# Two stacked transformer blocks on one core: the steps of all engines in another order, with matmuls on one part of the array more often together

## The reference

```python
def first_block(x, ...):
    for layer in range(2):
        h = rms_norm(x, pre_norm[layer])
        m = even_mixer(h, ...) if layer % 2 == 0 else odd_mixer(h, ...)
        x = x + rms_norm(m, post_norm[layer])

def even_mixer(h, positions, w_in, w_out):
    (aq, ak, av, ag, iq, ik, iw, bq, bk, bv, bg) = split_columns(h @ w_in, EVEN_WIDTHS)
    a = dsa_attention(...) * jax.nn.silu(ag)
    r = head_group_norm(retention(...)) * jax.nn.silu(bg)
    return jnp.concatenate([a, r], axis=-1) @ w_out
```

## Time and profile before

| | |
|---|---|
| time, median of 3 runs | 866.23 us (866.14 to 866.57) |
| span of the profiled execution, first to last instruction | 864.6 us |
| TensorE, matmuls | 855.4 us busy, 99% of the span |
| TensorE, weight loads (beside matmuls) | 725.5 us |
| VectorE | 671.9 us, 78% |
| ScalarE | 489.5 us, 57% |
| GpSimd | 40.3 us, 5% |
| transfers | 155.12 MB, 179 GB/s on average |
| granted TensorE clock | 0.999 of full speed |

### The profile page before, as it was taken

The page is one execution under the profiler, slowest core; times in us unless marked ns, Lnnn a source line. Parts: engine busy times, 40 slices in busy tenths (PEclk is TensorE's granted clock), DMA queues, the critical chain, the costliest instruction groups (busy, mean ns, idle before and its releaser), DMA issues.

```text
span 864.6 us, 13438 instructions
## 1 busy us (share of the span) xinstructions
PE 855.4 (99%) x5062; PEld 725.5 (84%) x5062; DVE 671.9 (78%) x1238; ACT 489.5 (57%) x905; POOL 40.3 (5%) x72
## 2 busy tenths in 40 slices
...
GB/s 328 287 240 150 167 80 194 137 221 222 167 99 228 268 219 49 77 111 179 172 202 212 174 193 228 188 131 251 115 159 146 146 195 221 169 220 213 216 155 49
DMA packets 46748, 155.12 MB, mean 179 GB/s; under 512 B 5500, under 2 KB 8668, under 8 KB 46684
## 3 DMA queue, kind: packets, MB, share of 16 engines
...
...
## 4 chain that ended last, share of the span: by engine, by line
PE 97%; DVE 1%; ACT 1%; DMA 0%; issue 0%; SPq 0%; POOL 0%; DVEq 0%
PE ps L2161 17%; PE ps L2189 14%; PE ps L797 12%; PE ps L973 10%; PE ps L2169 9%; PE ps L809 6%; PE ps L861 5%; PE ps L872 4%; PE ps L864 4%; PE ps L1062 4%; PE ps L1119 3%; PE ps L1071 3%; PE ps L905 1%; PE ps L800 1%; PE ps L801 1%; DMA raw<-in_ws 0%
## 5 line engine op out<-in xcount | busy, mean ns | idle before, releaser
L769 DVE TENSOR_TENSOR wlo<-raw,whi 128x1024 fp32r<-128x1024 f32 (+1 forms) x262 | 311.1, 1216 | 56.6 <-ACT whi L762 55.3
L762 ACT ACTIVATE whi<-raw 128x1024 fp32r<-128x1024 f32 x261 | 266.6, 1049 | 115.9 <-DMA raw<-in_ws 37.1
L2161 PE MATMUL ps<-t,whi 128*128 128x512 f32 x640 | 156.1, 391 | 0.0
L2161 PEld LDWEIGHTS ps<-t,whi 128*128 128x128 f32 x640 | 117.7, 188 | 22.8
L797 PE MATMUL ps<-t,whi 128*128 128x512 f32 x432 | 109.3, 397 | 0.0
L2189 PE MATMUL ps<-whi,r 128*128 128x512 f32 x352 | 95.4, 391 | 0.0
L797 PEld LDWEIGHTS ps<-t,whi 128*128 128x128 f32 x432 | 78.2, 188 | 17.3 <-issue 1.8
L2169 PEld LDWEIGHTS ps<-t,wlo 128*128 128x128 f32 x640 | 84.7, 191 | 4.7
L2169 PE MATMUL ps<-t,wlo 128*128 128x256 f32 x640 | 86.4, 283 | 0.0
L2189 PEld LDWEIGHTS ps<-whi,r 128*128 128x128 f32 x352 | 64.6, 188 | 12.2
L809 PEld LDWEIGHTS ps<-t,wlo 128*128 128x128 f32 (+1 forms) x472 | 62.5, 189 | 4.2 <-issue 0.3
...
## 6 DMA issues: line engine op xcount, KB each, us to landing
...
```

Source lines behind the costliest of these rows:

```text
L762: a.i.activation(whi[:, j % NSPLIT, 0:n], raw[:, j % NRAW, 0:n], ACT.Copy).then_inc(*a.sig("hi", u))
L769: d.i.tensor_tensor(wlo[:, j % NSPLIT, 0:n], raw[:, j % NRAW, 0:n], whi[:, j % NSPLIT, 0:n].bitcast(F), ALU.subtract).then_inc(*d.sig("lo" ...
L2161: p.i.matmul(ps[:, b, :], wh[:, k, :], t2[:, k, :], start=k == 0, stop=False)
```

## The change

Only `ORDER` changes: in all seven sections the lists of TensorE, ACT, DVE and GpSimd have the same steps as before in another order. Nothing is added or taken away, SP's list stays, and the table is 15 lines longer, so line 1062 of before is line 1077 of after, and so on for all lines behind the table. On TensorE the steps `log` and `val` stand next to each other more often. Most other steps move as well, by a few places.

Of the table, a line or two at the places spoken of below:

```diff
     start=dict(
         act=listed("""
-        T 0 0 0, hi 1, T 0 1 0, hi 1, T 0 0 1, T 0 1 1, hi 1, hi 1, vec 0, hi 1, sq pre0 0 0, sq pre0 0 1, hi 1, half mk0 0, sq pre0 1 0,
+        T 0 0 0, hi 1, vec 0, hi 1, T 0 1 0, T 0 0 1, hi 2, T 0 1 1, vec 1, hi 1, sq pre0 0 0, sq pre0 0 1, hi 1, sq pre0 1 0,
...
     ffn0=dict(
         pe=listed("""
-        chunk f_in0_0 2 1, clow f_in0_0 2 1, chunk f_in0_0 3 1, clow f_in0_0 3 1, jt 0, up 0 1 0, up 0 1 1, ulow 0 1 0, ulow 0 1 1,
+        chunk f_in0_0 2 1, clow f_in0_0 1 1, clow f_in0_0 2 1, clow f_in0_0 3 1, up 0 1 0, jt 0, ulow 0 1 0, up 0 1 1,
```

More of the change, by code:

```diff
@@ L257 @@
         pe=listed("""
[L258 to L269, removed]
@@ L275 @@
[L275 to L278, removed]
@@ L285 @@
[L285 to L288, removed]
@@ L290 @@
+        xw e 0 0, xw e 0 1, lo 2, row pre1 0 0, row pre1 0 1, lo 1, T 3 0 0, gain post0 1 0, gain post0 1 1, xw e 1 0, xw e 1 1,
+        T 3 0 1, lo 1, row pre1 1 0, row pre1 1 1"""),
         pool=listed("""
@@ new lines @@
+        tlow o_q 2, tlow o_q 1, tile o_q 3, tlow o_q 3, uq 0, uq 1, uq 2, uq 3, ukv 0, ukv 1, ukv 2, ukv 3, log l0, tile o_dg 0,
+        tlow o_dg 0, log l1, tile o_dg 1, log l2, tlow o_dg 1, tile o_dg 2, tile o_dg 3, tlow o_dg 3, turn l0 0, tile o_k 0,
+        tlow o_dg 2, turn l1 1, turn l0 1, tlow o_k 0, tile o_k 1, tlow o_k 1, turn l2 0, turn l1 0, tile o_k 3, tile o_k 2,
+        tlow o_k 2, turn l2 1, tlow o_k 3, val l0, log x0, chunk o_cg 0 0, val l1, log x1, chunk o_cg 1 0, clow o_cg 1 0,
@@ L328 @@
         pe=listed("""
-        chunk a_v 0 0, clow a_v 0 0, chunk a_v 1 0, clow a_v 1 0, T 5 1 0, T 5 1 1, chunk a_v 0 1, chunk a_v 1 1, clow a_v 0 1,
-        clow a_v 1 1, tile a_c 0, tlow a_c 0, tile a_c 1, tlow a_c 1, tile a_qm 0, tlow a_qm 0, tile a_qm 1, tlow a_qm 1, w1 k 0, w1 k 1,
-        w1 k 2, log m0, tile a_q 0, tile a_q 1, log m1, tlow a_q 0, tlow a_q 1, turn m0 0, turn m0 1, w1 k 3, w1 v 0, w1 v 1, w1 v 2,
-        w1 v 3, log n0, tile a_q 2, tlow a_q 2, log n1, comp1, tile a_q 3, tlow a_q 3, turn m1 0, turn m1 1, log n2, val m0, comp3,
@@ new lines @@
+        clow a_v 1 1, tile a_c 0, tlow a_c 0, tile a_c 1, tlow a_c 1, tile a_qm 0, tlow a_qm 0, tile a_qm 1, tlow a_qm 1,
+        w1 k 0, w1 k 1, w1 k 2, w1 k 3, log m0, tile a_q 0, tlow a_q 0, tile a_q 1, turn m0 0, turn m0 1, tlow a_q 1, log m1,
+        val m0, w1 v 0, w1 v 1, w1 v 2, w1 v 3, log n0, turn m1 0, tile a_q 2, turn m1 1, comp1, log n1, tile a_q 3, tlow a_q 2,
+        tlow a_q 3, comp3, log n2, turn n0 1, tile a_q 4, turn n0 0, tlow a_q 4, tile a_q 5, tlow a_q 5, val m1, log n3, cmps,
```

321 lines of the change are left out of this document (175 added, 146 removed).

## The result

The changed kernel takes 872.33 us (median of 4 runs, 872.21 to 873.05). Before, run beside it, took 866.19 (866.14 to 866.57). The ratio is 1.0069, interval 1.0054 to 1.0083: 6.1 us slower, where 865.4 was forecast and the range ended at 868.4. The profiled execution of after has a span of 870.5 us, 5.9 more than that of before, at the same granted clock (0.999).

The account below looks back on a forecast made before the run. The prediction took TensorE's matmuls, their extra costs and its waits as the bound. Terms -1.2 - 0.4 + 0.3 + 0.3 + 0.2 = -0.8 gave 864.6 - 0.8 + 1.6 = 865.4 us, range 863.0 to 868.4.

Parts of the forecast that it names:

- The bound: Whole kernel: 97% of the chain that ended last is TensorE, so time is its matmuls, their extra costs and waits.
- The switches: TensorE, all sections: 47 stretches of part-array steps become 38, less more alternations; -1.2 us, bounds -0.4 and -2.1.
- Inner joints: Inside part-array stretches: `val` then `log` costs +0.06 us, seven more of them +0.42; `log` then `val` is free.
- `jt 0`: Transposes at the start of `ffn0`: a step put ahead covers their late ACT copy, so a wait goes; -0.4 us.
- `T 5`: Transposes ahead of `nsa`: first chunk waits 0.83 us after `T 5 0`, `T 5 1` stops waiting 0.5; +0.3, bounds -0.1, +0.7.
- The head: Kernel start: ACT issues the `vec` loads earlier, which delays weight loads that TensorE needs; +0.3 us.
- Just in time: Some six places along the new order where a result comes within 0.2 us of its use; +0.2 us, bounds 0, +1.
- The mark that the prediction had set for this: More than 3 us of idle TensorE behind the head would make the sum wrong whatever the switches do.
- the six places named: `log l2`, `log x1`, `T 7 0 0`, `T 10 0 0`, `cmpt 0` and `chunk b_v0 3 0`, where results come just in time.
- ACT's casts ahead of its copies: Slower rival: at the starts of `moba`, `ffn0`, `ffn1`, casts delay copies, three by 1.06 us, +3.2; 868.6 us, chance 0.19.
- The sign set for this rival: Waits of TensorE on a cast (`whi`) behind the head would prove the slower rival.

Follow-up runs that it names:

- Run 8: After, with five places in ACT's and DVE's lists of `even` reordered and TensorE's list unchanged: 868.86 us, ratio 1.0027 against before.
- run 7: After, with the two `vec` loads put later in ACT's list of `start`: 873.5 us in one run.
- runs 4 and 5: In ACT's list of `even`: after, second `T 1 1` copy moved ahead of a waiting cast, 870.33 us; before, that cast put between the copies, 876.4 us.

## Why the prediction was wrong

The direction was wrong, by one term of the sum. Point by point:

- **The bound** was read rightly: the time is TensorE's sum plus its waits. I read from it, without a run of its own, why the loss is so large: ACT, DVE and the loads had time to spare only where the old order had put it.
- **The switches: -1.2.** Over the whole program the rest fell by 1.17, but that is partly chance: 0.92 of it is in `start`, where there are no switches and small waits became fewer and larger ones, and `even` rose by 1.02 with its ten stretches as before. Run 8, with the same TensorE list, has 0.46 of that left (1.11 less 0.65 of waits), so over half of it was waits too small for the other column; the 0.46 may be alternations. In the other sections, where all nine stretches vanished, the rest fell by 1.27 (53.20 to 51.93), 0.14 for each, most of it in `nsa`. For these sections the size holds, and with the 0.46 the term is some -0.8 by my estimate, inside the bounds; the spread over the sections wasn't foreseen (`moba` has two stretches fewer and is 0.23 up).
- **Inner joints.** A `val` ahead of a `log` was to show 1.09 us. It shows 1.10 with scores of 128 columns and 1.02, so nothing, with 256 columns. TensorE's timeline of after:

```profile
242.19 1.09 PE L1134 MATMUL ps<-pt,arena 128*64 128x128 f32 x16
243.29 1.16 PE L1077 MATMUL ps<-arena 64*128 64x128 f32 x16
244.38 0.73 PE L876 MATMUL ps<-whi,t 128*128 128x512 f32 x2
...
245.51 1.09 PE L1134 MATMUL ps<-pt,arena 128*64 128x128 f32 x16
246.53 1.13 PE L1077 MATMUL ps<-arena 64*128 64x256 f32 x8
247.60 0.73 PE L876 MATMUL ps<-whi,t 128*128 128x512 f32 x2
```

- **`jt 0`: -0.4.** Right. Where there was a wait, the eight transposes now take 0.79 us:

```profile
406.73 1.03 PE L2166 MATMUL ps<-ident,arena 128*128 128x128 f32 x8
407.52 0.72 PE L2184 MATMUL ps<-t,wlo 128*128 128x256 f32 x4
```

- **`T 5`: +0.3.** The mechanism was right on both sides: the first chunk waits (it starts 1.52 us behind the first of the eight transposes ahead of it, 0.65 over the price that I take for them), and `T 5 1` doesn't, its eight taking 0.80 us where they took 1.44. Waits went from 0.60 to 0.65, so the term is nearer +0.1.

```profile
287.15 1.03 PE L920 MATMUL ps<-ident,x 128*128 128x128 f32 x8
288.67 0.87 PE L876 MATMUL ps<-whi,t 128*128 128x164 f32 x6 [0.48 <-ACT t L926]
...
290.98 1.04 PE L920 MATMUL ps<-ident,x 128*128 128x128 f32 x8
291.78 0.44 PE L876 MATMUL ps<-whi,t 128*128 128x164 f32 x2
```

- **The head: +0.3.** `start` measured +0.57 in this run. Since it varies by more than that from run to run (run 7), the term is neither shown nor refuted.
- **Just in time: +0.2, bounds 0 and +1. This is the step that failed.** Without `jt 0`, `T 5` and the head, new waits came to some 6 us, of which 4.46 in `even`. The mark that the prediction had set for this, more than 3 us of idle TensorE behind the head, was passed. None of the six places named was the one. I had listed steps whose *input from the step before* comes late, with the durations of today's rows; where the new order puts ACT's casts was asked in the rival alone, and there at other places. But a cast doesn't run when its list reaches it; it runs when its load has come (at 42.29 us in before, 5.63 after ACT was free for it).
- **ACT's casts ahead of its copies** was a rival, with 0.19. Its mechanism is what happened (runs 4 and 5). Its place was wrong: at the start of `moba` the forecast pattern is there, ACT waits 4.16 us for a load with a copy behind it, and it costs TensorE 0.29 us of idle time (0.45 over the price).

```profile
588.77 1.06 ACT L777 ACTIVATE whi<-raw 128x1024 fp32r<-128x1024 f32 x1 [4.16 <-DMA raw<-in_ws]
589.74 0.58 ACT L2321 ACTIVATE arena<-ps 128x512 f32<-128x512 f32 x1
```

Its price was wrong too. I put 1.06 us on each such cast, the length of the instruction; the price is the wait of the cast for its load (up to 5.6 us), less what covers it, plus the feedback: a late copy holds DVE's subtraction, which frees the buffer of the next load, for which the next cast waits. The number was in my rows: the longest of ACT's 34 waits was 5.6 us, and I used it only to say that TensorE hadn't noticed. It stands at 42.29 us, right behind the two copies between which the new list puts that cast. I never asked where it was. The sign set for this rival, TensorE waiting on a cast (`whi`) behind the head, would have missed it: both such waits of after, 1.4 and 0.4 us, end in the head, at 6.98 and 15.64 us; behind it TensorE waits on copies and on DVE's results that stand behind the casts.

The Trainium skill (TensorEngine Tiling (Array Packing), Key Properties) was weighed for its rule "Mode switching requires drain". By it a joint inside a stretch is a switch like its ends. The rows above agree for `val` ahead of scores of 128 columns, with a cost of 0.07 us (1.10 against 1.03 alone), and differ for 256 columns (1.02 us), so the measurement decides: at some joints the change of form is free.
